# Four norms moved behind the first products of their sections: unscaled split tiles first, scaled parts swapped in

## The reference

```python
def rms_norm(x, g):
    y = x * lax.rsqrt(jnp.mean(x * x, axis=-1, keepdims=True) + 1e-6)
    return y * g

h = rms_norm(x, mix_norm_g)                 # norm 0
u, q, kv, nsa_g, merge_g = split(h @ w_in)  # pooling mixer on u, three-branch attention on q, kv
x = x + (gate_pool * y_pool + gate_nsa * y_nsa) @ w_out
h = rms_norm(x, ffn_norm_g)                 # norm 1
gate_pre, val = split(h @ w_up)
x = x + (silu(causal_dwconv(gate_pre)) * val) @ w_down
for l in range(2):
    h = rms_norm(x, norm_g_2[l])            # norms 2 and 3
    ... = split(h @ w_in_2[l])              # among them iq, ik, iw, bq, bk: an indexer and attention
    x = x + merged @ w_out_2[l]
```

## Time and profile before

| | us |
|---|---|
| median of 3 runs | 2183.5 (2183.08 to 2184.16) |
| profiled execution, its own time | 2182.32 |
| its span | 2180.5 |
| PE busy in the span | 2073.7 |
| DVE, ACT, POOL busy | 1141.7, 892.0, 335.2 |

### The profile page before, as it was taken

How to read it: one execution, slowest core, us unless ns; L and a number is a source line. 1 busy time by engine, 2 the same in 40 slices (tenths; PEclk the granted TensorE clock), 3 DMA queues, 4 the chain that set the end, 5 groups by cost and what they waited for, 6 DMA issues and landing times. The chain is left out here.

```text
span 2180.5 us, 29393 instructions
## 1 busy us (share of the span) xinstructions
PE 2073.7 (95%) x11739; PEld 1764.3 (81%) x11747; DVE 1141.7 (52%) x1809; ACT 892.0 (41%) x1452; POOL 335.2 (15%) x178
## 2 busy tenths in 40 slices
PE   5999999889999998999999999999999999999997
PEld 5977777678787777898898798877798899788886
DVE  3656564246355364479445655442479545565452
ACT  4345455233333234343444445333443344545341
POOL 1010000212012021035110010220134201010210
PEclk9999999979999997999999999998999999999999
DMA  4211111313222223222122022223122212122221
GB/s 169 97 64 41 57 55 62 116 41 108 83 96 80 94 96 116 78 78 97 59 78 97 27 85 90 93 97 116 58 78 97 72 65 97 39 71 88 97 96 58
DMA packets 24308, 179.09 MB, mean 82 GB/s; under 512 B 2816, under 2 KB 3456, under 8 KB 3712
## 3 DMA queue, kind: packets, MB, share of 16 engines
q1 hardware_dynamic: 22752, 164.24, 22.1%
q10 hardware_dynamic: 1440, 13.24, 1.6%
HBM read 171.18 MB, written 6.29 MB: 81 GB/s over the span
## 5 line engine op out<-in xcount | busy, mean ns | idle before, releaser
L248 DVE TENSOR_TENSOR wlo<-wraw,whi 128x2048 fp32r<-128x2048 f32 x128 | 296.3, 2316 | 365.0 <-ACT whi L243 364.4
L254 PE MATMUL pp<-hhi,whi 128*128 128x512 f32 (+1 forms) x1096 | 444.3, 405 | 12.1 <-POOL hlo L450 11.9
L256 PE MATMUL pp<-hhi,wlo 128*128 128x512 f32 (+1 forms) x1096 | 432.2, 394 | 0.0
L255 PE MATMUL pp<-hlo,whi 128*128 128x512 f32 (+1 forms) x1096 | 431.9, 394 | 0.0
L254 PE MATMUL pp<-whi,hhi 128*128 128x256 f32 x1344 | 394.5, 294 | 0.2
L255 PE MATMUL pp<-wlo,hhi 128*128 128x256 f32 x1344 | 381.8, 284 | 0.0
L256 PE MATMUL pp<-whi,hlo 128*128 128x256 f32 x1344 | 381.5, 284 | 0.0
L243 ACT ACTIVATE whi<-wraw 128x2048 fp32r<-128x2048 f32 x152 | 289.6, 1906 | 0.0
L254 PE MATMUL pp<-split,whi 128*128 128x512 f32 x624 | 254.8, 408 | 23.9 <-POOL split L2193 10.0
L254 PEld LDWEIGHTS pp<-whi,hhi 128*128 128x128 f32 x1344 | 259.2, 193 | 12.9 <-issue 7.2
L255 PEld LDWEIGHTS pp<-wlo,hhi 128*128 128x128 f32 x1344 | 259.2, 193 | 0.5
(11 more groups left out here) (347 smaller groups left out, 2560.5 us busy)
## 6 DMA issues: line engine op xcount, KB each, us to landing
wraw<-weights SPq DMA_DIRECT2D x152, 1024.0 KB, 4.8
out_t<-xT ACTq DMA_DIRECT2D x2, 2048.0 KB, 6.3
xT<-out_t ACTq DMA_DIRECT2D x2, 2048.0 KB, 8.3
xT<-x_t SPq DMA_DIRECT2D x1, 2048.0 KB, 7.6
work<-cmp_w ACTq DMA_DIRECT2D x1, 2048.0 KB, 7.4
xT<-x_t ACTq DMA_DIRECT2D x1, 2048.0 KB, 8.2
out_t<-xT SPq DMA_DIRECT2D x1, 2048.0 KB, 6.3
work<-small ACTq DMA_DIRECT2D x3, 128.0 KB, 4.8
```

Source lines behind the costliest of these rows:

```text
L248: nc.vector.tensor_tensor(wlo[:, slot, :], wraw[:, slot, :], whi[:, slot, :].bitcast(F32), ALU.subtract).then_inc(w_lo, 1)
L254: nc.tensor.matmul(out_ap, ah, bh, start=start, stop=False)
L255: nc.tensor.matmul(out_ap, ah, bl, start=False, stop=False)
L256: return nc.tensor.matmul(out_ap, al, bh, start=False, stop=stop)
```

## The change

Each norm is taken apart. What feeds the first four dense tiles (u; up0's first two chunks; iq) is now g times x, unscaled: ACT writes `hhi` = round(g x) and DVE `hlo` = g x - `hhi`, for each k as soon as x is there (for norms 1 to 3 inside `act_out` and `dve_out`, which replace the evacuation of wout, down2 and layer 0's wout2). POOL adds up the eight squares, so that TensorE has one group of one-column products instead of eight, behind the first tile; the spreading stands behind the second. During the fourth tile (for layers, the ikg tile) ACT and DVE put the scaled parts in the place of the unscaled ones, k by k (`act_swap`, `dve_normed`, `dve_swap`). Results of the unscaled tiles are scaled afterwards: u by one DVE instruction, the first two rounds of up0 by four, ikg by one, and iq inside the relu's scale.

Besides: the first loads are ordered anew (vectors, chunk 0, constants, x in four pieces, masks, positions, chunk 1); in up0 the list `FF_ORDER` says after which iteration `act_ff` is done; DVE's pooling windows move behind other work; POOL makes the low parts of three more chunks in each layer (ikg and both of bq); x is saved in two transfers per layer and the result is stored in four.

```diff
+        def norm_at(n, slot):
+            return (2048, 12288)[n > 0] + 512 * slot
+        def squares(n, k):
+            return wv(norm_at(n, 2), S) if k == 0 else wv(norm_at(n, k % 2), S)
+        def normed(n, k):
+            return wv(8192 + 512 * k, S) if n == 1 else xT[:, k, :]
+        def swap_tile(n):
+            name, l, at = (("u", None, 3), ("up0", None, 3), ("ikg", 0, 0), ("ikg", 1, 0))[n]
+            return section(name, l)[2] + at
+        def act_raw(act, n, k):
...
+            nc.scalar.activation(hhi[:, k, :], xT[:, k, :], ACT.Copy, scale=gain(n, k)).then_inc(xg_hi, 1)
+            if k >= 3:
+                act.wait_ge(sq_acc, 7 * n + k - 2)
+            nc.scalar.activation(squares(n, k), xT[:, k, :], ACT.Square).then_inc(sq_ready, 1)
+            if n >= 2 and k % 4 == 3:
+                act.dma_start(out[:, k - 3:k + 1, :], xT[:, k - 3:k + 1, :]).then_inc(x_kept, 16)
+        def dve_raw(dve, n, k):
+            dve.wait_ge(xg_hi, KT * n + k + 1)
+            nc.vector.scalar_tensor_tensor(out=hlo[:, k, :], in0=xT[:, k, :], scalar=gain(n, k),
+                                           in1=hhi[:, k, :].bitcast(F32), op0=ALU.mult,
+                                           op1=ALU.subtract).then_inc(xg_lo, 1)
+        def pool_squares(pool, n):
+            acc = squares(n, 0)
+            for k in range(1, KT):
+                pool.wait_ge(sq_ready, KT * n + k + 1)
+                pool.drain()
+                nc.gpsimd.tensor_tensor(acc, acc, squares(n, k), ALU.add).then_inc(sq_acc, 1)
+        def pe_raw(pe, n, name, l, j):
...
+            for x in range(KT):
+                if j == 0:
+                    pe.wait_ge(xg_lo, KT * n + x + 1)
+                last = three(pp[(par0 + j) % 2][:, :], (wh[:, x, cc], wl[:, x, cc]), (hhi[:, x, :], hlo[:, x, :]),
+                             x == 0, x == KT - 1)
+                if t0 + j == swap_tile(n) and x < KT - 1:
+                    last.then_inc(h_free, 1)
+            last.then_inc(mm_done, 1)
+            if j == 0:
+                pe.wait_ge(sq_acc, 7 * (n + 1))
...
+                last.then_inc(ss_done, 1)
+            if j == 1:
+                pe.wait_ge(inv_ready, n + 1)
...
+                last.then_inc(inv_spread, 1)
+        def act_swap(act, n, k):
...
+            act.wait_ge(t_ready, KT * n + k + 1)
+            nc.scalar.activation(hhi[:, k, :], normed(n, k), ACT.Copy).then_inc(nrm_hi, 1)
+        def dve_normed(dve, n):
+            dve.wait_ge(inv_spread, n + 1)
+            for k in range(KT):
+                nc.vector.scalar_tensor_tensor(out=normed(n, k), in0=xT[:, k, :], scalar=gain(n, k), in1=ps[1][:, :],
+                                               op0=ALU.mult, op1=ALU.mult).then_inc(t_ready, 1)
+        def dve_swap(dve, n):
+            for k in range(KT):
+                dve.wait_ge(nrm_hi, KT * n + k + 1)
+                nc.vector.tensor_tensor(hlo[:, k, :], normed(n, k), hhi[:, k, :].bitcast(F32),
+                                        ALU.subtract).then_inc(nrm_lo, 1)
+        def act_out(act, name, l, dst, norm):
...
+                nc.scalar.activation(dst[:, n, :], pp[(par0 + n) % 2][:, :], ACT.Copy).then_inc(evac, 1)
+                act_raw(act, norm, n)
+                if n % 2 == 1:
+                    act_next(act, name, l, c0 + n // 2, (slot0 + n // 2) % 2)
+        FF_ORDER = [[], [], [0], [1], [2], [3, 4], [5], [6]]
...
-            pool.wait_ge(w_lo, c0 + 2)
-            for k in range(12):
+            pool.wait_ge(w_lo, c0 - 1)
+            for k in range(-3, 12):
                 low_part(c0 + k + 2)
...
             dve_next(dve, "ksw", None)
+            dve_window(dve, 3, WINDOWS[3])
             for x in range(2):
...
+                gated = FF_ORDER if r == 0 else [[]] + [[k] for k in range(ROUNDS[r] - 1)]
...
-                    if k >= 1:
-                        act_ff(act, r, k - 1)
+                    for j in gated[k]:
+                        act_ff(act, r, j)
...
-            sp.wait_ge(stage["dve"], stage_no["dve"])
-            sp.dma_start(out, xT[:, :, :]).then_inc(out_done, 16)
+            for k in range(4):
+                sp.wait_ge(x_ready, 5 * KT + 2 * k + 2)
+                sp.dma_start(out[:, 2 * k:2 * k + 2, :], xT[:, 2 * k:2 * k + 2, :]).then_inc(out_done, 16)
```

More of the change, by code:

```diff
@@ L233, in pairs @@
             elif n >= 2:
-                with eng.Fori(0, n) as j:
+                with eng.Fori(first, n) as j:
                     body(j)
@@ L265, in pe_tile, with pe_fm @@
             product(pp[par]).then_inc(mm_done, 1)
-        def pe_fm(pe, name, l, h, kt, cols, ready=None, last_late=False, only=None):
+        def pe_fm(pe, name, l, h, kt, cols, ready=None, last_late=False, only=None, first=0):
             c0, n, t0, per = section(name, l)
@@ new lines, in pe_raw @@
+        def pe_raw(pe, n, name, l, j):
+            c0, _, t0, per = section(name, l)
+            par0, slot0 = par_of(name, l)
+            k, m = j // per, j % per
+            if m == 0:
+                pe.wait_ge(w_lo, c0 + k + 1)
+            if t0 + j >= 2:
+                pe.wait_ge(evac, t0 + j - 1)
+            wh, wl = weights((slot0 + k) % 2, KT, 256)
+            cc = slice(m * P, m * P + P)
+            for x in range(KT):
[8 more added lines that the diff above has]
+                pe.wait_ge(sq_acc, 7 * (n + 1))
+                for i in range(QT):
+                    last = nc.tensor.matmul(ps[0][:, i:i + 1], squares(n, 0)[:, P * i:P * i + P], ones[:, 0:1],
+                                            start=(i == 0), stop=(i == QT - 1))
+                last.then_inc(ss_done, 1)
+            if j == 1:
+                pe.wait_ge(inv_ready, n + 1)
+                for i in range(QT):
+                    last = nc.tensor.matmul(ps[1][:, i * P:i * P + P], ones, wv(norm_at(n, 3) + P * i, P), start=True,
+                                            stop=True)
+                last.then_inc(inv_spread, 1)
@@ L402, in act_norm, with act_root @@
+        def act_root(act, n):
+            act.wait_ge(ss_done, n + 1)
             nc.scalar.activation(stat[:, 40:44], ps[0][:, 0:QT], ACT.Sqrt, scale=1.0 / D,
                                  bias=con(C_EPS)).then_inc(root_ready, 1)
[L404 to L418, removed]
+        def act_swap(act, n, k):
+            if k < KT - 1:
+                act.wait_ge(h_free, 7 * n + k + 1)
+            else:
+                act.wait_ge(mm_done, swap_tile(n) + 1)
+            act.wait_ge(t_ready, KT * n + k + 1)
+            nc.scalar.activation(hhi[:, k, :], normed(n, k), ACT.Copy).then_inc(nrm_hi, 1)
@@ L763, in selected, with pe_tm_tile @@
             return (0, selm[:, OFF[i]:OFF[i] + P * (i + 1)]) if i else (0, msk[:, M_CH:M_CH + P])
-        def pe_tm_tile(pe, name, l, n, first=0, end=KT):
+        def pe_tm_tile(pe, name, l, n, first=0, end=KT, ready=None):
             c0, _, t0, _ = section(name, l)
@@ L1147, in act_layer @@
         def act_layer(act, l):
-            act_norm(act, 2 + l)
-            c0, n, t0, per = section("iq", l)
+            n0 = 2 + l
+            c0, _, t0, _ = section("iq", l)
             par0, slot0 = par_of("iq", l)
@@ L1738, in _ @@
             pe_fm(pe, "wout", None, mr, KT, 256, lambda x: pe.wait_ge(m_lo, x + 1))
-            pe_norm(pe, 1)
+            for j in range(4):
+                pe_raw(pe, 1, "up0", None, j)
             for r in range(3):
-                pe_fm(pe, f"up{r}", None, h, KT, 256, h_ready(pe, 1) if r == 0 else None)
+                pe_fm(pe, f"up{r}", None, h, KT, 256, h_ready(pe, 1) if r == 0 else None, first=(r == 0))
                 pe_fm(pe, f"down{r}", None, mr, ROUNDS[r], 256,
```

290 lines of the change are left out of this document (177 added, 113 removed).

## The result

The changed kernel takes 2150.8 us, the median of four runs (2149.95 to 2151.55), against 2183.7 us for the kernel before (also four runs, 2183.08 to 2184.16). The ratio is 0.985, with a 95% interval of 0.983 to 0.987. The profiled execution took 2149.95 us where the one before took 2182.32, so 32.4 us are to be found.

A forecast was written before the change was run, and what follows sets the result against it. TensorE, busy 95% of the span, was taken as the bound, with time lost at the norms. Terms -10.8 + 1.6 - 6.5 - 9.8 - 3.4 = -28.9 gave 2153.4 profiled, median 2154.6 us; 8-in-10 range 2135 to 2170.

The forecast's parts named there:

- the likeliest case: Whole kernel: the terms hold as summed, with errors of a few us each; 2145 to 2165 us, chance 0.55.
- Start: Norm 0 through vsw: cmp ends 17.9 us earlier; 0.3, 4.4 and 2.4 us given back; -10.8 us.
- hold-up in vsw: First tile of vsw: window 3 delays ACT's root and evacuation; TensorE waits 4.4 us, plus 2.4 of clock.
- Norm 1: Between wout and up0: hole -25.7, added products 1.8, three sigmoid-order stalls 18.3, clock 7.2; +1.6 us.
- Norm 2: Down2 into a layer: hole -25.7, added products 1.8, swap held up 11.8, clock 2.2, down2 3.4; -6.5 us.
- The port's part: In each layer, POOL's conversions hold up DVE's two-SBUF-operand swap subtractions, delaying the indexer; 11.8 us.
- Norm 3: The other layer's norm: hole -25.6, added products 1.8, swap held up 11.8, clock 2.2; -9.8 us.
- End: Output store: last piece of 0.5 MB lands in 2.9 us against 6.3 for 2 MB; -3.4 us.
- B: Layers: the port does not hold the swap up, 14.6 us less; 2140 us, chance 0.13.
- C: Up0: no stall, because some wait lets the sigmoid go earlier, 25.5 us less; 2129 us, chance 0.08.
- D: Swap late at the start or in up0, or down2 at its upper bound; 2162 to 2170 us, chance 0.18.
- E: Six waits each leave TensorE at 1.2 GHz for 24 us, 58 more; 2213 us, chance 0.04 slower, 0.02 draw.

## Why the prediction was right

The forecast was 2154.6 us, the result 2150.8, in the range of the likeliest case. By its own terms:

- **Start, -10.8; measured -10.7 at wout's end.** The parts are a little off in both directions, and it is luck that they cancel. cmp ends 17.5 us earlier (17.9 forecast). The one-column products ran at the high clock and took 0.9 us where 1.7 stood, while the masks' cast began at 13.32 and not 12.8 and the sums came 1.6 us apart and not 1.5. The hold-up in vsw cost 5.8 and not 6.8, since the low spell took 1.5 and not 2.4. Between vsw and wout 0.6 us were lost that the forecast did not have: a low spell in mg was longer (13.7 us for 10.2), and merge1 gave only part of that back. Moving the window gave the 5.8 back, and moving the cast took another 3.2 off the start. What was missing was that the masks held the first tile's own roundings up.
- **Norm 1, +1.6; measured +1.63.** The waits are 6.17, 6.02 and 6.12 us where three of 6.1 stood. The clock cost 6.7 in place of 7.2. That leaves 23.4 for the hole less what was added, where 23.9 stood, and the two small errors cancel. Undoing norm 1 gave 1.6 us back in its section.
- **Norm 2, -6.5; measured -8.5** (down2, iq and bq). Down2 was mis-sized: some 2.2 us were lost there and in iq, not 3.4 (three times 1.0 to 1.1 is in any case 3.0 to 3.3), for the three conversions were late by 0.14, 0.70 and 0.54, and the norm's own parts by 0.38 and 0.22. The port's part was 11.4 (15.4 us from ikg's end to the indexer against 3.9) where 11.8 stood, and the clock 1.8 for 2.2.
- **Norm 3, -9.8; measured -9.8.** The agreement is closer than its parts. The port cost 11.4 here too where 11.8 stood, and the clock 2.6 for 2.2.
- **End, -3.4; measured -3.7.** The last piece landed in 2.6 us, inside the bounds of 1.6 and 4.0. The Trainium skill's sum (DMA: Bandwidth & Descriptors, "Anatomy of one DMA") gives 3.2 us for such a piece, for transfers that GpSimd issues; these are SP's, the trace has less, and the trace decides.
- **Not forecast:** -1.3 in down1, where the kernel before had a low spell of 6.8 us and the changed one of 3.4 at the same wait.

These add up to -32.4; the forecast had -28.9. The difference is norm 2 (2.0) and down1 (1.3).

Of the rivals, B (the port holds nobody up) is refuted by the 4.67 and 4.99 us members and by the experiment that moved one conversion. The row of a single instruction in the earlier trace rows did hold for a stream of eight: one subtraction is caught by each conversion, and the rest go at their pace. With the rule that the prediction cited from the Trainium skill (SBUF — State Buffer, "Who interferes with whom") the rows agree in both directions, though for the second they show only 0.3 us. POOL's second conversion met a subtraction under way and took 4.89 us, against 4.60 for the first and 4.51 for the one in the experiment that began with no such subtraction under way. C (no wait in up0) is refuted by the rows. D (the swap late at the start or in up0, down2 at its upper bound) did not come: in up0 the first subtraction ends at 445.62 and tile 4 starts at 446.62, 1.0 us to spare where 0.8 stood. E (a clock that stays low for 24 us behind each wait) did not come for the up0 waits, whose spells are 6.8 us. It came nearest in the layers, where the clock was low for 17 us, but there TensorE had little to do in most of them.

## What to carry to other kernels

Hiding a norm behind products pays only if nothing that those products need stands behind a wait of the new order. Here one conversion of weights, written behind a wait for a sigmoid, took the whole gain of a norm back, and moving it ahead of the wait returned it. When the instructions of two engines hold each other up, as POOL's conversions and DVE's subtractions do here, the long one should not lie beside the chain of short ones on which TensorE waits. Here each meeting cost nearly the length of the long one, some 4 of its 4.6 us. A wait of TensorE costs more than its length, here about 2.2 us on top of 6.1, so that it is worth counting waits and not only adding them up.

## What was not expected of the hardware

Twenty-four products of no use, issued in each wait, kept the granted clock at 1.00 and saved 6.7 us in the section, though they did nothing for the wait itself. In the layers, where TensorE did 44 small products in 16.9 us between waits, it stayed at 0.50. The same waits in the same place were followed by low spells of different length from one execution to the next (6.8 us behind up0's third wait in one trace, 10.2 in another), which moves the whole kernel by about 1 us each and limits what its times can tell apart.
